# Streaming-encoder block: sums of x on TensorE, shift and scale matrices by chunk in slot pairs, head units cut unit by unit

## What is computed

```python
def rms_norm(x, g):
    xf = x.astype(jnp.float32)
    y = xf * lax.rsqrt(jnp.mean(xf * xf, axis=-1, keepdims=True) + EPS)
    return y.astype(x.dtype) * g

def modulate(n, shift, scale):
    return n * (1.0 + scale[:, None, :]) + shift[:, None, :]

def swiglu(n, w_in, w_out):
    hu = n @ w_in                                   # (B, S, 2*D_FF)
    h, u = jnp.split(hu, 2, axis=-1)
    return (jax.nn.silu(h) * u) @ w_out             # (B, S, D)
...
    ada = (jax.nn.silu(c) @ w_ada + b_ada).reshape(bsz, N_ADA, 3, D_MODEL)
    h = x
    for _ in range(DEPTH):
        n = modulate(rms_norm(h, g_ffn1), ada[:, 0, 0], ada[:, 0, 1])
        h = h + 0.5 * ada[:, 0, 2][:, None, :] * swiglu(n, w1_in, w1_out)
```

## Time and profile before

| what | value |
|---|---|
| median of 3 runs | 2609.82 us (2609.46 to 2749.47) |
| profiled execution | 2607.45 us |
| its span, slowest core (5) | 2605.9 us |
| spans of the 8 cores | 2601.9 to 2605.9 us |
| mean granted TensorE clock | 0.989 to 0.995 |
| TensorE busy | 96% of the span |
| VectorE, ScalarE, GpSimd busy | 39%, 16%, 12% |
| HBM read | 546.09 MB |

### The profile page before, as it was taken

How to read it: one execution, slowest core, us unless ns; L and a number is a source line. 1 busy time by engine, 2 the same in 40 slices (tenths; PEclk the granted TensorE clock), 3 DMA queues, 4 the chain that set the end, 5 groups by cost and what they waited for, 6 DMA issues and landing times.

```text
span 2605.9 us, 38186 instructions; the slowest of 8 cores (2601.9 to 2605.9 us)
## 1 busy us (share of the span) xinstructions
PE 2508.5 (96%) x14754; PEld 1408.2 (54%) x14754; DVE 1022.3 (39%) x1488; ACT 429.6 (16%) x771; POOL 304.4 (12%) x572
## 2 busy tenths in 40 slices
PE   1899999999999999999999999999999999999997
PEld 0566666666666666577544444444444444444445
DVE  5467545444455446647732224611021010210126
ACT  3422000000000013523511111500000000000013
POOL 1220211111111111000110100000000000000002
PEclk9999999999999999999999999999999999999998
DMA  9999998999998995743384553354444444444436
GB/s 232 161 165 207 188 172 144 155 158 160 163 153 141 167 156 115 150 93 66 75 187 81 90 100 57 65 97 81 74 80 73 81 73 74 81 75 73 67 61 166
DMA packets 104321, 310.07 MB, mean 119 GB/s; under 512 B 12240, under 2 KB 26960, under 8 KB 104016
## 3 DMA queue, kind: packets, MB, share of 16 engines
q0 software_dynamic: 79024, 260.12, 61.5%
q1 hardware_dynamic: 25120, 47.50, 5.7%
HBM read 546.09 MB, written 16.78 MB: 216 GB/s over the span
## 4 chain that ended last, share of the span: by engine, by line
PE 90%; DMA 4%; DVE 2%; ACT 2%; issue 1%; DVEq 0%; POOL 0%; SPq 0%; ACTq 0%; POOLq 0%
PE ps L275 90%; DMA ring<-w_head 2%; ACT nT L285 2%; DMA hT<-xT 1%; DVE U L289 1%; DMA ring<-w_out 1%; DVE rs L306 1%; DVE hT L300 0%; ACT L285 0%; DVE hT L289 0%; ACT rs L285 0%; POOL ring L322 0%; DVEq L1088 0%; SPq L337 0%; ACTq L1088 0%
## 5 line engine op out<-in xcount | busy, mean ns | idle before, releaser
L275 PE MATMUL ps<-nT,ring 128*128 128x352 bf16 (+3 forms) x9344 | 1652.6, 339 | 17.4 <-ACT nT L285 9.7
L275 PEld LDWEIGHTS ps<-nT,ring 128*128 128x128 bf16 x9344 | 912.8, 98 | 743.6 <-issue 30.5
L275 PE MATMUL ps<-U,ring 128*128 128x352 bf16 (+3 forms) x4480 | 800.7, 340 | 3.2 <-DMA ring<-w_out 3.2
L275 PEld LDWEIGHTS ps<-U,ring 128*128 128x128 bf16 x4480 | 437.1, 98 | 356.1 <-issue 4.8
L285 ACT ACTIVATE tmp<-ps 128x512 f32<-128x512 f32 (+1 forms) x268 | 142.6, 534 | 1709.4 <-PE ps L275 1674.4
L289 DVE TENSOR_TENSOR U<-tmp,ps 128x352 bf16<-128x352 f32 (+1 forms) x190 | 113.1, 597 | 771.9 <-PE ps L275 760.8
L300 DVE SCALAR_TENSOR_TENSOR hT<-ps,ghT,hT 128x352 f32<-128x352 f32 (+3 forms) x288 | 183.0, 636 | 367.3 <-PE ps L275 367.2
L385 DVE SCALAR_TENSOR_TENSOR ring<-ring,rs 128x2048 bf16<-128x2048 bf16 x112 | 253.0, 2285 | 12.2 <-DMA ring<-w_adaD 12.2
L322 POOL DMA_DIRECT2D ring<-w_in x212 | 112.5, 532 | 1195.4 <-PE ps L275 1178.4
L322 POOL DMA_DIRECT2D ring<-w_out x118 | 62.4, 530 | 563.4 <-PE ps L275 554.5
L285 ACT ACTIVATE nT<-hT 128x512 bf16<-128x512 f32 (+4 forms) x138 | 79.3, 583 | 201.6 <-DVE hT L300 190.5
(11 more groups left out here) (65 smaller groups left out, 570.1 us busy)
## 6 DMA issues: line engine op xcount, KB each, us to landing
ring<-w_in POOLq DMA_DIRECT2D x212, 512.0 KB, 6.6
ring<-w_adaD POOLq DMA_DIRECT2D x112, 512.0 KB, 10.9
ring<-w_out POOLq DMA_DIRECT2D x80, 512.0 KB, 6.2
hT<-xT SPq DMA_DIRECT2D x8, 2112.0 KB, 23.4
ring<-w_ada POOLq DMA_DIRECT2D x32, 512.0 KB, 18.1
ring<-w_out POOLq DMA_DIRECT2D x38, 384.0 KB, 5.9
hscr<-hT SPq DMA_DIRECT2D x16, 512.0 KB, 8.5
hT<-hscr SPq DMA_DIRECT2D x16, 512.0 KB, 13.2
```

Source lines behind the costliest of these rows:

```text
L275: e.matmul(o, l, r, start=st, stop=sp, skip_group_check=sk),
```

## The change

- x and its reload lie in DRAM as [128, 16, 1056], so that a group of four chunks is one row of 16.9 KB for each partition, where it was four rows of 4.2 KB.
- The squares go to `nT` (14 on ACT, chunks 13 and 15 on DVE), and three bf16 matmuls for each chunk sum them, accumulating in PSUM over the 16 chunks; the additions on DVE go. A dummy Sqrt on ACT stands ahead of the squares. Each block gets its root, and `x_scale` for chunks 0 and 1 is done block by block between the reciprocals.
- w_ada lies by chunk: item "a i" is now both tiles of chunk i, in one transfer of 1 MB to a pair of slots. Pairs are slots 0 and 1, 2 and 3, 4 and 5 in turn. `ada_mm` runs for both and `ada_cols`, `x_scale`, `x_mod` follow every item.
- Pieces of units use slots 6 to 9 in turn. Units 0 to 2 are cut in five pieces, 3 to 7 in four, 8 and 9 in three; `HEAD_ORDER` is new.

```diff
-KCUTS = ((0, 4), (4, 7), (7, 11), (11, 16))
+CUTS_A = ((0, 2), (2, 4), (4, 7), (7, 11), (11, 16))
+CUTS_B = ((0, 4), (4, 8), (8, 11), (11, 16))
+CUTS_C = ((0, 7), (7, 11), (11, 16))
+KCUTS = [CUTS_A] * 3 + [CUTS_B] * 5 + [CUTS_C] * 2
 HEAD_ORDER = (
-    "a0 a1 a2 a3 a4 a5 a6 a7 u0.0 u1.0 a8 u2.0 a9 u3.0 "
...
-    "a28 u8.2 a29 u9.2 a30 a31 u0.3 u1.3 u2.3 u3.3 u4.3 u5.3 u6.3 u7.3 "
-    "u8.3 u9.3 "
+    "a0 a1 u0.0 u1.0 u2.0 a2 a3 u0.1 u1.1 u2.1 u3.0 a4 u4.0 u5.0 "
...
+    "u7.2 a14 u8.1 u9.1 a15 u0.4 u1.4 u2.4 u3.3 u4.3 u5.3 u6.3 u7.3 u8.2 "
+    "u9.2 "
 ).split()
...
-                in_=xT[g4 * 512:(g4 + 1) * 512, :].rearrange("(k p) t -> p k t", p=P)),
+                in_=xT[:, g4 * 4:(g4 + 1) * 4, :]),
...
+        dummy = adaT[:, 143:144]
+        op_act(dummy, ones32D[:, 0:1], AF.Sqrt, [("ones32D", 0, 1)], [Bada.r(0, 143, 144)])
+        st_bank = [new_bank() for _ in TB3]
         for kc in KALL:
-            sq_acc(kc, 0, T, kc == 0)
-
-        rms_stats(TB3)
+            if kc >= 12 and kc % 2 == 1:
+                op_tt(nT[:, kc, :], hT[:, kc, :], hT[:, kc, :], ALU.mult, [Bh.r(kc)], [Bn.r(kc)])
+            else:
+                op_act(nT[:, kc, :], hT[:, kc, :], AF.Square, [Bh.r(kc)], [Bn.r(kc)])
+            for bk, (x, y) in zip(st_bank, TB3):
+                op_mm(psum[bk][:, 0:y - x], ones_rms[:], nT[:, kc, x:y], kc == 0, kc == KC - 1,
+                      reads=[("ones_rms", 0, 1), Bn.r(kc, x, y)], writes=[psr(bk)])
+        NPRE = 2
+        for bk, (x, y) in zip(st_bank, TB3):
+            rms_root(bk, x, y)
+            for kc in range(NPRE):
+                op_tt(hT[:, kc, x:y], hT[:, kc, x:y], rs[:, x:y], ALU.mult, [Bh.r(kc, x, y), Brs.r(0, x, y)], [Bh.r(kc, x, y)])
...
             if item[0] == "a":
-                return fill_kc(w_ada[int(item[1:])])
+                kc = int(item[1:])
+                s = 2 * (kc % 3)
+                first_rd = [Bh.r(11)] if not slot_used else []
+                slot_used.append(s)
+                S.add("pool", lambda e: e.dma_start(out=ring[:, s:s + 2, :].rearrange("p a b -> p (a b)"),
+                                                    in_=w_ada[kc], max_dma_last_dim=8192),
+                      reads=first_rd, writes=[slot_r(s), slot_r(s + 1)], dma=("slot", s))
+                return s
...
-            return fill_slot([(w1_head[u][:, 2 * P * k0:2 * P * k1], 1, 2 * P * n, 0)])
+            s = 6 + head_ctr[0] % 4
+            head_ctr[0] += 1
+            return fill_slot([(w1_head[u][:, 2 * P * k0:2 * P * k1], 1, 2 * P * n, 0)], s)
...
-            for kc in range(4):
+            for kc in range(NPRE, 4):
                 x_scale(kc)
...
-                    ada_mm(16 * (i % 2) + i // 2, sl)
-                    if i % 2 == 1:
-                        ada_cols(i // 2)
-                        if i // 2 + 4 < KC:
-                            x_scale(i // 2 + 4)
-                        x_mod(i // 2)
+                    ada_mm(i, sl)
+                    ada_mm(16 + i, sl + 1)
+                    ada_cols(i)
+                    if i + 4 < KC:
+                        x_scale(i + 4)
+                    x_mod(i)
```

More of the change, by code:

```diff
@@ L154, in build_nc @@
     nc = bass.Bass("TRN2", target_bir_lowering=False)
-    xT = nc.dram_tensor("xT", [D, T], F32, kind="ExternalInput").ap()
+    xT = nc.dram_tensor("xT", [P, KC, T], F32, kind="ExternalInput").ap()
     ppd = nc.dram_tensor("pp", [P, NPP], F32, kind="ExternalInput").ap()
-    w_ada = nc.dram_tensor("w_ada", [32, P, KC, P], F32, kind="ExternalInput").ap()
+    w_ada = nc.dram_tensor("w_ada", [KC, P, 2 * D], F32, kind="ExternalInput").ap()
     w_adaD = nc.dram_tensor("w_adaD", [112, P, D], F32, kind="ExternalInput").ap()
@@ L888, in park @@
             return Buf(hT[:, c:c + 1, :], "h", c * T * 4, T, 4)
+        head_ctr = [0]
         def head_fill(item):
             if item[0] == "a":
-                return fill_kc(w_ada[int(item[1:])])
+                kc = int(item[1:])
[6 more added lines that the diff above has]
+                return s
             u, p = (int(v) for v in item[1:].split("."))
-            k0, k1 = KCUTS[p]
+            k0, k1 = KCUTS[u][p]
             n = k1 - k0
-            return fill_slot([(w1_head[u][:, 2 * P * k0:2 * P * k1], 1, 2 * P * n, 0)])
+            s = 6 + head_ctr[0] % 4
+            head_ctr[0] += 1
+            return fill_slot([(w1_head[u][:, 2 * P * k0:2 * P * k1], 1, 2 * P * n, 0)], s)
         def ffn1_head():
             late = []
-            LASTP = len(KCUTS) - 1
             def run_late(keep):
@@ L915, in x_reload @@
                 S.add("sp", lambda e: e.dma_start(
-                    out=hT[:, c0:c1, :], in_=xT[c0 * P:c1 * P, :].rearrange("(k p) t -> p k t", p=P)),
+                    out=hT[:, c0:c1, :], in_=xT[:, c0:c1, :]),
                     writes=[Bh.rr(c0, c1)], dma=("xr", key))
-            for kc in range(4):
+            for kc in range(NPRE, 4):
                 x_scale(kc)
@@ L924, in ffn1_head @@
                     i = int(item[1:])
-                    ada_mm(16 * (i % 2) + i // 2, sl)
-                    if i % 2 == 1:
-                        ada_cols(i // 2)
-                        if i // 2 + 4 < KC:
-                            x_scale(i // 2 + 4)
-                        x_mod(i // 2)
+                    ada_mm(i, sl)
[4 more added lines that the diff above has]
+                    x_mod(i)
                     continue
                 u, p = (int(v) for v in item[1:].split("."))
-                k0, k1 = KCUTS[p]
+                k0, k1 = KCUTS[u][p]
+                last = len(KCUTS[u]) - 1
                 n = k1 - k0
@@ L947, in ffn1_head @@
                             op_act(pa, psum[bk][:, 0:w], AF.Copy, [psr(bk)], [pr])
-                        elif p < LASTP or hu == 1:
+                        elif p < last or hu == 1:
                             op_tt(pa, psum[bk][:, 0:w], pa, ALU.add, [psr(bk), pr], [pr])
@@ L953, in ffn1_head @@
                             op_act(tmp[:, ti, 0:w], tmp[:, ti, 0:w], AF.Silu, [Btmp.r(ti, 0, w)], [Btmp.r(ti, 0, w)])
-                    if p == LASTP:
+                    if p == last:
                         def fin(u=u, x=x, y=y, w=w, ti=ti, pa=pa, pr=pr):
@@ L1140, in _prep_inputs @@
     wa = np.asarray(inp["w_ada"], dtype=np.float32)
-    wa_t = np.ascontiguousarray(tile_cols(wa[:, :4096]).reshape(2, KC, P, KC, P).transpose(1, 0, 2, 3, 4)).reshape(32, P, KC, P)
+    wa_t = np.ascontiguousarray(tile_cols(wa[:, :4096]).reshape(2, KC, P, KC, P).transpose(1, 2, 0, 3, 4)).reshape(KC, P, 2 * D)
     wa_d = np.ascontiguousarray(wa[:, 4096:].T).reshape(112, P, D)
@@ L1147, in _prep_inputs @@
     for u in range(NHEAD):
-        for (k0, k1) in KCUTS:
+        for (k0, k1) in KCUTS[u]:
             n = (k1 - k0) * P
@@ L1205, in _prep_inputs @@
         ppv[:, C_ID:C_ID + CHB] = np.tile(np.eye(CHB, dtype=np.float32), (NPH, 1))
-        m = {"xT": np.ascontiguousarray(xs[PERM].T), "pp": ppv,
+        m = {"xT": np.ascontiguousarray(xs[PERM].T.reshape(KC, P, T).transpose(1, 0, 2)), "pp": ppv,
              "cbc": np.ascontiguousarray(np.broadcast_to(c[b][None, :], (P, D)))}
```

## The result

The changed kernel takes 2634.14 us (median of 5 runs, four of them 2632.87 to 2635.16); beside it the kernel before took 2609.46 us. The ratio is 1.0085 with an interval of 1.0068 to 1.0103: about 22 us slower, with 18 to 27 us as the interval, and 25 us as the difference of the medians. This lies beyond the predicted range (2604 to 2624), though within the 2% called no change. In some runs one half of the chip had a lower granted clock and took longer; the ratios leave these out, and so do the medians given for the experiments.

What follows compares the result with a forecast made beforehand. Transfers were taken to set the pace up to the first w_out tile, at 323.9 us. Terms -1.5 (head), +9 (four slots), -1 (reload) gave +6.5 us, a forecast median of 2616 us, range 2604 to 2624.

Steps and rivals of the forecast that it cites:

- What bounds the head: First 324 us: transfers set the pace; TensorE's work before 189 us counts only if it changes transfer starts or speed.
- Sums and first unit: Start of the head: first unit near 55 us for 64.10; 9 us gained for TensorE, 0 for the head's end.
- x in one row: Load and reload of x: longer rows gain 1.5 us for the head and 1 us for the reload.
- Pairs and pieces: w_ada by chunk, pieces by unit, in the head: value 0 if the queue never runs dry before a15; other bound 3 us.
- Four slots for the last pieces: Behind the head, 194 to 217 us: w_in waits behind last pieces, 12 us idle against 3.4 now; price 9 us.
- Sum: First w_out tile at 330.4 us for 323.9, nothing changed behind it: +6.5 us on the whole.
- The rival with larger transfers: Head: fewer, larger transfers run faster, a15 lands 10 us sooner, sum -3.5 us, 2606 us; chance 0.18.
- The rival at 2630: Head: TensorE's restarts after waits are paid, twenty more cost 33 us against 19 us of slack; chance 0.06.

Runs made afterwards that it cites:

- the ring of ten: Changed kernel's order and cuts, but all ten slots in turn for everything, each w_ada pair as two one-slot transfers: 2608.58 and 2608.70 us.
- cbc late: Kernel before, with only the 1 MB cbc table held until unit 2 has ended: 2615.52 us for 2618.11, ratio 0.9996 (0.9979 to 1.0013).
- the two ring kernels: Changed order, ten slots in turn: throughout (2608.58, 2608.70 us), or up to a15 with four for the last pieces (2628.28, 2629.82, 2648.71 us, ratio 1.0081).

## Why the prediction was right and where it was wrong

**What bounds the head.** Right. The sums alone gave no time, the ring of ten started its first unit 12.7 us sooner and gained nothing at the last pieces, and 12 us of added work on TensorE moved the end by nothing that shows. The transfers set the pace.

**Sums and first unit.** The first unit was said for 55 us and came at 51.29; "9 us for TensorE, 0 for the end of the head" held in its second half, where it counted. Of the 3.7 us more, 3.3 come from x, whose last group landed 4.3 us sooner on the cores shown (32.18 for 36.57) instead of 1.

**x in one row.** Taken as 1.5 us for the head and 1 us for the reload; neither is contradicted. On the kernel before, the part is worth 2.5 us at the last pieces in the trace of one core and 0.9 us by the median over the cores; the interval of the ratio, 15 us faster to 4 slower, can't say more. In the changed kernel nothing of it shows in the time (old rows: 1.0099 against 1.0098); that it is lost in the holes behind is likely but was not isolated.

**Pairs and pieces.** This step failed: "Value: 0 if the queue never runs dry before a15". The working looked at the bytes in flight at the start and said that "later the queue holds one pair at least". The slots speak otherwise. GpSimd works in order, so a piece that waits for one of four slots holds up the pair behind it (a8, for 19 us), and the windows from 70 to 80, 100 to 120 and 160 to 180 us lose (1.05 - 0.85) / 1.05 x 10, (1.05 - 0.94) / 1.05 x 20 and (1.05 - 0.93) / 1.05 x 20 us, 6.3 us in all, where 3 was the named bound. The last pieces started at 197.33 us for 188 predicted. With a ring of ten and order and cuts unchanged it is 190.26, so the divided ring costs about 7 us there. At the end it is 6 to 7 us: 2614.96 against 2608.64 us with ten slots for the last pieces, 2635.65 against 2629.05 with four, each time with only two runs of the ring kernel.

**Four slots for the last pieces.** The mechanism was right, each sign of it was found: the share near 0.5, w_in issued late, new waits for w_in, none of it left with ten slots. The term was mis-sized: 9 us predicted, 18.9 measured on one chip. Its working has two errors. First, the stretch: the sketch had 23 us with the queue short of work, from 194 to 217, and it was 32, from 200 to 232. The first last piece took 6.9 us instead of 4.5 (197.33 to the issue at 204.25, at a granted clock of 0.86), the transfers in flight were through 3 us after 197 and not 6, and from the first w_in issue (227.14) it took some 5 us until the share was full again (0.85 from 228 to 232 us) and not 2. The three windows above give a mean share of 0.51 in it, so (1 - 0.51 / 1.05) x 32 = 16.5 us are idle, where the prediction had 12. Second, it deducted 3.4 us as lost before too; with slots in the order in which they come free nothing is lost there (1.05 from 204 to 220 us), so against that version the price is the whole. By bytes moved instead of busy share, the stretch loses more: it moves 67 GB/s where the ten-slot kernel moves 168 from 200 to 232 us, so (1 - 67 / 168) x 32 = 19.2 us. By the first count 18.9 - 16.5 = 2.4 us remain, of the size of TensorE's slower matmuls behind the w_in waits (96 in 17.26 us at 250 us for 14.48 fifty us later); by the second nothing remains. No run decides between the two.

The kernel before with four slots lost 13.4 us by its ratio, on another chip where it is slower by itself. Why this is 5 to 6 us less stays open; with the old x rows the changed kernel is no nearer (2636.24 us for 2635.65), and the slower chip isn't excluded. There is no trace of the kernel before on that chip; the nearest is that with cbc late, whose first w_out matmul lies between 326.72 and 331.37 us on its cores, already later than on the first chip, against 341.85 to 348.55 with four slots: 18 us by the medians (328.59 and 346.44).

**Sum.** The last pieces +7.7 us (predicted -1.5), from there to the first w_out matmul 151.7 us for 134.4, +17.3 (predicted +8), and next to nothing behind it (1.7 us), as predicted. 25.0 us for 6.5 up to w_out. Seen from TensorE, waits for w_in and w_out are 13.3 us of the middle part, for 3.2 before (about 10 were predicted); the rest of the 17.3 us is mostly the same matmuls at a lower granted clock, 0.93 for 0.99 from 236 to 360 us. The DMA share is 1.03 in that stretch in both kernels, which speaks for the transfers as the pace there too, but no run separates the two. The row of before, to be set beside that of the changed kernel above:

```profile
236.00:360.00 124.00, 120.81 (x800) 78.59 (x798) 61.91 (x75) 10.13 (x19) 19.04 (x36) 0.99 1.03 196
```

**Transfers twice as large.** The rival with larger transfers (2606) would have had to bring the last pieces below 180 us; they came later. In the two ring kernels each pair is two transfers again, and the share is 1.05 as with 62 transfers before; and where the changed kernel's queue has no hole, from 140 to 160 us, its pairs move 164 GB/s, where the single tiles of before move 167. The Trainium skill, "DMA: Bandwidth & Descriptors", section "Anatomy of one DMA — SWDGE (gpsimd) path", has a fixed cost of about 2.0 us for each transfer; with about six in flight at a time, an estimate from the 18.1 us to landing and 3.2 us of bytes each, these runs show none of it in the pace.

**Restarts.** The rival at 2630 was nearest to the number, for another reason than its own. The added matmuls and the ten-slot kernels, whose clock in the head is as low (0.84 and 0.87) and which lose nothing like 25 us, speak against it for the head. Its own working allowed 19 us of slack; the clock was low in that slack. What the low clock costs behind the w_in waits is open, as said.

**Which bound was too narrow.** The range took 9 us and 0 us as nearly certain sizes. Idle time of a full resource is set by the queue that refills it; with 12 us from a sketch of issue times, 20 would have been the honest upper end, and the pairs' 3 us bound was borrowed from another gap and not worked out from this queue's waits for slots.

## What to carry to other kernels

Where an in-order queue feeds a full resource, count slots and not bytes: write down for each transfer what it waits for, and look for the first one that stands before others whose slots are empty. Dividing a ring by kind of tile costs nothing in bytes, and 19 us here where ten tiles of one kind follow one another through four slots; handing slots out in the order in which they come free gave most of it back. In a stretch that is already at a full share, look for bytes to move out (cbc: 3 us on one chip, though the interval against the kernel before still touches no change) before making its compute faster, which gave nothing that shows here. And compare all cores: the time is that of the slowest, and a loss can fall on some alone.

## What the runs showed of the hardware

- x in rows of 16.9 KB moves hardly faster than in rows of 4.2 KB, with all eight cores loading it: from 8 to 26 us 320 to 331 GB/s in the changed kernel, 317 to 323 before. The last of the four groups, which shares the engines with w_ada, lands at 31.65 to 33.03 us on the eight cores, before at 33.74 to 36.57; on one chip with nothing else changed it is 31.85 to 33.24 against 32.32 to 35.73.
- The same program differs between chips of the kind by 9 us (medians 2609.5 to 2618.1 for the kernel before). The one trace close to it on the slowest chip, with cbc late, shows waits for w_in (2.9 us in all, the first tile issued at 281.07) that the kernel before doesn't have on the first chip; chip or edit, that isn't separated.
- A w_in tile issued behind the reload and eight w_in and w_adaD tiles takes 41.93 us from issue to landing, against a median of 18 for w_ada in the head and at most 33.5 for any ring tile before.
- After the waits for w_in the granted clock is below full: 0.71 from 250 to 260 us, 0.86 from 270 to 280, and 1.00 again from 280 on. 96 matmuls take 17.26 us, where 96 take 14.48 some 50 us later:

```profile
250.07 17.26 PE L277 MATMUL ps<-nT,ring 128*128 128x352 bf16 x96 [3.70 <-DMA ring<-w_in]
...
303.35 14.48 PE L277 MATMUL ps<-nT,ring 128*128 128x352 bf16 x96 [0.45 <-DMA ring<-w_in]
```
